# Gate and up matmuls over both parts of x, with other reads and weight loads, in a two-block transformer kernel

## The reference, cut to what matters

```python
def swiglu(x, w_gate, w_up, w_down):
    return (jax.nn.silu(x @ w_gate) * (x @ w_up)) @ w_down
...
    for l in range(DEPTH):
        h = h + 0.5 * swiglu(rmsnorm(h, ffn1_norm[l]), ffn1_w_gate[l], ffn1_w_up[l], ffn1_w_down[l])
        ...
        h = h + 0.5 * swiglu(rmsnorm(h, ffn2_norm[l]), ffn2_w_gate[l], ffn2_w_up[l], ffn2_w_down[l])
```

## Time and profile before

| | us |
|---|---|
| median of 3 runs | 1557.85 |
| lowest, highest | 1557.55, 1558.78 |
| the profiled execution, its own time | 1558.99 |
| span of the profile | 1557.2 |
| TensorE busy | 1538.7 (99%) |
| VectorE busy | 1086.0 (70%) |
| ScalarE busy | 798.4 (51%) |
| mean granted TensorE clock | 0.998 |
| read from HBM | 257.83 MB, 166 GB/s |

### The profile page before, as it was taken

How to read it: one execution, slowest core, us unless ns; L and a number is a source line. 1 busy time by engine, 2 the same in 40 slices (tenths; PEclk the granted TensorE clock), 3 DMA queues, 4 the chain that set the end, 5 groups by cost and what they waited for, 6 DMA issues and landing times.

```text
span 1557.2 us, 29379 instructions
## 1 busy us (share of the span) xinstructions
PE 1538.7 (99%) x12818; PEld 1506.6 (97%) x12818; DVE 1086.0 (70%) x1490; ACT 798.4 (51%) x1029; POOL 44.5 (3%) x43
## 2 busy tenths in 40 slices
PE   7999999999999999999999999999999999999998
PEld 6999999999999999999999999999999999999988
DVE  6665588787875555755568778876688698666844
ACT  5344355565454334533355556444555645775653
POOL 0000001210000000000001010000000000000000
PEclk9999999999999999999999999999999999999999
DMA  7555545434455554555544443446555453325531
GB/s 279 190 185 189 169 153 171 140 132 147 171 198 184 177 183 169 208 180 177 186 153 156 176 136 136 154 171 247 189 182 172 163 190 113 132 82 192 181 129 55
DMA packets 38559, 260.76 MB, mean 167 GB/s; under 512 B 4640, under 2 KB 5024, under 8 KB 8864
## 3 DMA queue, kind: packets, MB, share of 16 engines
q1 hardware_dynamic: 37712, 257.84, 48.0%
q10 hardware_dynamic: 720, 1.05, 0.2%
HBM read 257.83 MB, written 1.05 MB: 166 GB/s over the span
## 4 chain that ended last, share of the span: by engine, by line
PE 92%; DVE 4%; ACT 2%; DMA 1%; issue 0%; ACTq 0%; DVEq 0%
PE ps L203 28%; PE ps L205 28%; PE ps L204 28%; DVE w_low L193 2%; ACT w_high L186 1%; PE ps L1210 1%; DMA w_raw<-in_weights 1%; PE ps L1222 1%; PE ps L1999 0%; PE ps L1982 0%; PE ps L1195 0%; PE ps L1202 0%; PE ps L1194 0%; PE ps L2424 0%; PE ps L1293 0%
## 5 line engine op out<-in xcount | busy, mean ns | idle before, releaser
L193 DVE TENSOR_TENSOR w_low<-w_raw,w_high 128x2048 fp32r<-128x2048 f32 (+2 forms) x245 | 554.6, 2265 | 203.4 <-ACT w_high L186 203.1
L186 ACT ACTIVATE w_high<-w_raw 128x2048 fp32r<-128x2048 f32 (+2 forms) x245 | 460.3, 1880 | 431.9 <-PE ps L205 425.6
L203 PE MATMUL ps<-x_high,w_high 128*128 128x256 f32 x2312 | 662.0, 286 | 11.5 <-DVE w_low L658 9.9
L204 PE MATMUL ps<-x_low,w_high 128*128 128x256 f32 x2312 | 654.7, 283 | 0.0
L205 PE MATMUL ps<-x_high,w_low 128*128 128x256 f32 x2312 | 654.7, 283 | 0.0
L203 PEld LDWEIGHTS ps<-x_high,w_high 128*128 128x128 f32 x2312 | 443.4, 192 | 17.3 <-issue 13.4
L204 PEld LDWEIGHTS ps<-x_low,w_high 128*128 128x128 f32 x2312 | 443.7, 192 | 0.9 <-issue 0.5
L205 PEld LDWEIGHTS ps<-x_high,w_low 128*128 128x128 f32 x2312 | 443.6, 192 | 0.0
L205 PE MATMUL ps<-ffn_hid_high,w_low 128*128 128x256 f32 x704 | 197.9, 281 | 0.0
L203 PE MATMUL ps<-ffn_hid_high,w_high 128*128 128x256 f32 x704 | 197.3, 280 | 0.0
L204 PE MATMUL ps<-ffn_hid_low,w_high 128*128 128x256 f32 x704 | 195.8, 278 | 0.0
(11 more groups left out here) (431 smaller groups left out, 1971.1 us busy)
## 6 DMA issues: line engine op xcount, KB each, us to landing
w_raw<-in_weights SPq DMA_DIRECT2D x230, 1024.0 KB, 4.9
w_raw<-in_weights SPq DMA_DIRECT2D x10, 768.0 KB, 4.2
even_second_vectors<-in_second SPq DMA_DIRECT2D x1, 1836.0 KB, 9.3
w_raw<-in_weights SPq DMA_DIRECT2D x3, 512.0 KB, 3.7
w_raw<-in_weights SPq DMA_DIRECT2D x2, 640.0 KB, 3.9
resid<-in_x SPq DMA_DIRECT2D x4, 256.0 KB, 5.5
w_raw<-in_weights ACTq DMA_DIRECT2D x4, 256.0 KB, 7.2
out<-resid SPq DMA_DIRECT2D x3, 256.0 KB, 2.4
```

What stands on the lines that cost most here:

```text
L186: act.activation(self.wh[:, j, 0:SIZES[n]], self.raw[:, j, 0:SIZES[n]], ACT.Copy).then_inc(self.hi_made, 1)
L193: dve.tensor_tensor(self.wl[:, j, 0:SIZES[n]], self.raw[:, j, 0:SIZES[n]], self.wh[:, j, 0:SIZES[n]].bitcast(F32), ALU.subtract).then_inc( ...
L203: pe.matmul(out, ah, bh, start=start, stop=False, skip_group_check=True)
L204: pe.matmul(out, ah, bl, start=False, stop=False, skip_group_check=True)
```

## The change

Five things are done.

- `x_high` and `x_low` become two halves of one tensor `x`, and gate and up slots use a new `wide`: the high weights move both halves, 512 columns, into a whole bank, and the low weights move `x_high`, 256 columns, into its first half. The two feature halves of a slot take a bank each: gate banks 0 and 1, up banks 2 and 3. The reader (`take_wide`) adds a bank's two halves with a reduce over pairs; the multiply by the scale is an operation of its own behind it, and at step 0 the reciprocal stands between them. The mean of a feed-forward's norm goes to bank 7. The side products of `Tables` wait until up's banks have been read, and their own readers are waited for before the next up (`taken`).
- SyncE issues slot 1 in two halves once the first two pieces of x and slot 0 have landed, and slot 2 once all four have; slot 1 is split in halves.
- In the even layer, at slot 8, `scan` stands ahead of the split.
- The first two output slots of the odd layer run heads 0 to 2 of both, and then head 3 of both.
- A feed-forward's first matmul waits for three residual adds of the unit before, not two.

```diff
-        self.xh = sb("x_high", [P, DT, SEQ], F32R)
-        self.xl = sb("x_low", [P, DT, SEQ], F32R)
+        self.x = sb("x", [P, 2, DT, SEQ], F32R)
+        self.xh, self.xl = self.x[:, 0], self.x[:, 1]
...
-        return n + PIECES
+        return n + PIECES + (n > 0)
...
+def take_wide(c, dve, out, bank):
+    return dve.tensor_reduce(out, c.ps[:, bank:bank + 2, :].rearrange("p f (a t) -> p f t a", a=2), AX.X, ALU.add)
+def wide(c, pe, bank, n, norm=None, midway=None):
+    wh, wl = c.weights_at(n, DT, FC)
+    if n > 1:
+        pe.wait_ge(c.lo_made, c.made(n))
+    for k in range(DT):
+        if midway and k == DT // 2:
+            midway()
+        if norm and k % 2 == 0:
+            pe.wait_ge(*norm.x_low(k // 2 + 1))
+        if n == 0 and k % 2 == 0:
+            pe.wait_ge(c.lo_made, k // 2 + 1)
+        if n == 1 and k % 4 == 0:
+            pe.wait_ge(c.lo_made, PIECES + 1 + k // 4)
+        for i in range(2):
+            f = slice(i * P, (i + 1) * P)
+            pe.matmul(c.bank(bank + i).rearrange("p (a t) -> p a t", a=2), wh[:, k, f], c.x[:, :, k, :], start=(k == 0),
+                      stop=False, skip_group_check=True)
+            mm = pe.matmul(c.bank(bank + i, SEQ), wl[:, k, f], c.xh[:, k, :], start=False, stop=(k == DT - 1),
+                           skip_group_check=True)
+    return mm
...
-B_GATE, B_UP, B_DOWN = (0, 2), 1, 4
+B_GATE, B_UP, B_DOWN, B_FFN_SUM = 0, 2, 4, 7
...
             dve.wait_ge(*self.filled(gate_at(s) + 1))
-            dve.tensor_tensor(b.gate[:, :, :], c.halves(B_GATE[s % 2]), scale, ALU.mult).then_inc(b.gate_read, 1)
+            take_wide(c, dve, b.gate[:, :, :], B_GATE).then_inc(b.gate_read, 1)
+            if s == 0:
+                self.norm.reciprocal(dve)
+            dve.wait_ge(*self.gate_read(s + 1))
+            dve.tensor_tensor(b.gate[:, :, :], b.gate[:, :, :], scale, ALU.mult).then_inc(b.gate_scaled, 1)
         def up(s):
             dve.wait_ge(*self.filled(up_at(s) + 1))
             if s:
                 dve.wait_ge(*self.hid_low(s))
-            dve.tensor_tensor(b.up[:, :, :], c.halves(B_UP), scale, ALU.mult).then_inc(b.up_read, 1)
+            take_wide(c, dve, b.up[:, :, :], B_UP).then_inc(b.up_read, 1)
+            dve.wait_ge(*self.up_read(s + 1))
+            dve.tensor_tensor(b.up[:, :, :], b.up[:, :, :], scale, ALU.mult).then_inc(b.up_scaled, 1)
...
-            if s >= 2:
-                pe.wait_ge(*self.gate_read(s - 1))
-            project(c, pe, B_GATE[s % 2], base + gate_at(s), DT,
-                    norm=None if s else self.norm).then_inc(c.done, 1)
+            if s:
+                pe.wait_ge(*self.gate_read(s))
+            wide(c, pe, B_GATE, base + gate_at(s), norm=None if s else self.norm).then_inc(c.done, 1)
         def up(s):
             if s:
                 pe.wait_ge(*self.up_read(s))
-            project(c, pe, B_UP, base + up_at(s), DT,
-                    midway=None if s else lambda: self.norm.mean(pe)).then_inc(c.done, 1)
+            self.aside.taken(pe, s)
+            wide(c, pe, B_UP, base + up_at(s), midway=None if s else lambda: self.norm.mean(pe)).then_inc(c.done, 1)
...
-            pe.wait_ge(*self.before(2))
+            pe.wait_ge(*self.before(3))
...
-            self.aside.tensor(pe, s)
+            self.aside.tensor(pe, s, self.up_read(s + 1))
...
-        c.load(sp, 1)
+        sp.wait_ge(*self.arrived(1))
+        for b, s in enumerate((self.half_in, c.landed[1])):
+            sp.dma_start(self.half(c.raw, b), c.weights[1][:, b * SLOT // 2:(b + 1) * SLOT // 2]).then_inc(s, 16)
+        sp.wait_ge(*self.arrived(PIECES - 1))
         c.load(sp, 2)
...
-        c.split_high(act, 1)
+        for b, s in enumerate((self.half_in, c.landed[1])):
+            act.wait_ge(s, 16)
+            act.activation(self.half(c.wh, b), self.half(c.raw, b), ACT.Copy).then_inc(c.hi_made, 1)
...
-    def tensor(self, pe, s):
+    def taken(self, pe, s):
+        e = self.e
+        if s == 8:
+            pe.wait_ge(e.skip_made, 4)
+        if s in (9, 10):
+            pe.wait_ge(e.b_copied, s - 8)
+    def tensor(self, pe, s, up_read):
         c, e = self.c, self.e
+        if s in (7, 8, 9):
+            pe.wait_ge(*up_read)
...
-            pe.wait_ge(*((e.b_copied, 1) if part else (e.skip_made, 4)))
...
+            if n == A_Q:
+                scan(A_S5.index(n))
             if n:
                 after(n)
-            if n in A_S5:
+            if n in A_S5 and n != A_Q:
...
+        def heads(n, which):
+            b = odd_bank(n) if which[0] else bank_free(n)
+            wh, wl = c.weights_at(base + n, DT, FC)
+            pe.wait_ge(c.lo_made, c.made(base + n))
+            for h in which:
+                pe.wait_ge(self.o_low, h + 1)
+                for kk in (2 * h, 2 * h + 1):
+                    for i in range(2):
+                        f = slice(i * P, (i + 1) * P)
+                        mm = exact3(pe, c.halves(b)[:, i, :], wh[:, kk, f], wl[:, kk, f], o.oh[:, kk, :], o.ol[:, kk, :],
+                                    kk == 0 and i == 0, kk == DT - 1)
+            return mm
...
+            if n == G_OUT:
+                heads(n, range(3))
+                heads(n + 1, range(3))
+                heads(n, (3,)).then_inc(c.done, 1)
+                heads(n + 1, (3,)).then_inc(c.done, 1)
+                continue
+            heads(n, range(GLA_HEADS)).then_inc(c.done, 1)
```

65 lines of the change are left out of this document (33 added, 32 removed).

## The result

The changed kernel takes **1565.8 us** (median of 5 runs, 1564.1 to 1567.78), the kernel before, beside it, 1557.71. The ratio is 1.0052, with a 95% interval from 1.0037 to 1.0067: slower by 8.1 us, where 5.5 us less were forecast and the range ended at 1561.

A forecast was written before the change was run, and what follows sets the result against it. PE's stream was taken to bound the kernel. Terms: -12.0 - 2.6 - 1.4 + 7.2 + 1.6 + 1.7 + 0 = -5.5 us, giving 1553.5 profiled and 1552.4 for the median; range 1543.5 to 1561.

The forecast's parts named there:

- pairs: Gate and up slots: two 256-column matmuls become one of 512, 1408 times, each saving 8.5 ns; 12.0 us saved.
- even, S5 before the split: Even mixer's slot 8: rotation ahead of the split removes PE's 1.2 us stand and likely 1.6 of slow matmuls; 2.6 us saved.
- odd head: Odd layer: PE's 1.3 us stand for `odd_o_low` goes, hidden behind 36 products of the next slot; 1.4 us saved.
- fourth: the stands: Fourth feed-forward: VectorE falls behind, so PE stands 5.8 us before the S5 products, plus smaller waits; 7.2 us lost.
- fourth: the clock: Fourth feed-forward: after the 6 us stand PE's clock drops and 17 matmuls run slowly; 1.6 us lost.
- third's gate 1: Where one feed-forward follows another: gate 1 now waits for gate 0's read behind two splits; 1.7 us lost, once.
- start: Kernel start: gate 1 begins at 24.8 to 27.6 against 25.49, between 0.7 won and 2.1 lost; taken as 0.
- The price of a read: VectorE: each of 88 bank reads costs 1.22 us more for its reduce, 2.5 us a step; hidden in plain steps.
- D: Rival, chance 0.15: slower because the reduce is dear; at 2.3 us a read the kernel takes 1563.
- B: Rival, chance 0.20: VectorE holds PE nowhere for long, so 12.5 to 14.5 us are won; about 1544.
- C: Rival, chance 0.14: merging two matmuls saves only 2.5 to 5 ns each; sum -0.5 to +3.0, about 1559.
- E: Rival, chance 0.03: 512-column matmuls over two distant pieces start 0.24 us apart, saving nothing; +6.5, 1564.

The follow-up runs named there:

- r4: The kernel before with only the two small parts added: S5 inputs ahead of the even layer's split, last odd head last; 1554.99 us against 1557.74.
- r7: The changed kernel with gate and up of steps 4 to 10 of the fourth feed-forward, and the side products' waits, as before; 1557.28 us.
- r10: The changed kernel with unpaced loads, position and table loads behind slot 4's, and step 0's gate and up reduces ahead of slot 3's split; 1557.33 us.
- r6: The changed kernel with gate and up of the last step of each feed-forward as before, in 256-column matmuls and one multiply as read; 1559.64 us.
- r2: The changed kernel without SyncE's two waits at the start, so slots 1 and 2 are issued at once; 1562.93 us.
- r1: The changed kernel with the reduce of gate 0 ahead of the split of slot 3, in all four feed-forwards; 1560.93 us.
- r9: The changed kernel itself, unaltered, profiled a second time; 1565.86 us (two runs).
- r5: The changed kernel with x_high and x_low of one k-tile side by side, so a 512-column matmul moves one unbroken row; 1567.45 us.
- r3: The changed kernel with the first residual add ahead of VectorE's last split in each feed-forward; 1561.62 us.

## Why the prediction was wrong

The forecast was -5.5 us, the measurement +8.1, outside the range. Each term stands against the traces of the two kernels:

| term | forecast | traces | runs |
|---|---|---|---|
| pairs | -12.0 | -14.7 | |
| even, S5 before the split | -2.6 | -2.3 | r4: -2.75 |
| odd head | -1.4 | -1.8 | (both) |
| fourth: the stands | +7.2 | +6.1 | r7: -8.5 |
| fourth: the clock | +1.6 | +2.6, in part hidden | (with its end) |
| third's gate 1 | +1.7 | +2.2 | r10: -8.5 |
| start | 0 | +6.8 | (both) |
| the feed-forwards' ends | not named | +6.3 | r6: -6.2 |

The traces' terms sum to +5.2; the spans differ by 5.1. The fourth feed-forward's two terms are PE's account of it; since VectorE sets its time behind the stand, they can't be told apart beyond their sum.

**Right.** The price of a read, 1.22 us and 2.5 a step, taken from a reduce of another shape; no row reduced pairs or read its input from PSUM, so that it held is partly luck. What it does in the fourth feed-forward up to the stand: one stand of 5.6 against 5.8, before the S5 products, on up 7's read; the wait in `taken`, 0.8, did not come, while those ahead of gate 7 and up 7, forecast at 0.2 and 0.4, were 0.2 and 0.3. The wait at the third feed-forward's gate 1, 1.8 against 1.7. The two small parts. VectorE hidden in plain steps: the double slots of the first three feed-forwards show no wait for it in between.

**Wrong, first: the start** ("Gate 1 starts at 24.8 to 27.6 against 25.49 ... I take 0"). Gate 1 started at 29.55, 4.1 us later. Two steps failed. Slot 3's split was put between 23.6 and 26.4 because its load was issued earlier; it ended at 28.36, since an earlier place in a busy queue is not an earlier landing, and what had been held back to let the first pieces through was now ahead of it. And the sentence that PE waits elsewhere for the same thing compared the start of gate 1 with before, without asking what a stand of 6 us does to the clock: 2.7 us more, by the same reading of the clock that the prediction made for the fourth feed-forward. r2 puts 2.9 us down to the pacing, r1 shows that the order of VectorE's work is the other part, and r10, with both mended and the tables moved, leaves nothing of it; what the tables' place is worth alone was not run.

**Wrong, second: the ends of the feed-forwards.** The prediction asked of each place whether VectorE's work fits into a step, and wrote of the adds that they cost nothing "as long as VectorE adds in time". It did not follow the chain of the last step, which has no step behind it to catch up in. Its slack was in the trace: `x_low` at 201.94, PE at 202.88. Two reads at 1.26 against 0.94 gives 1.6 by that reading, and 1.6 from start to start was measured, four times. This term alone takes the forecast from -5.5 to +0.8.

**Wrong, but small: two sentences.** "By step 8 VectorE has used the stand to catch up": it had not, as the two profiles of the change show. And the whole difference was "applied to the median": the 1.6 us of slow matmuls in the even layer stand in the profiled execution and in about a quarter of the others, so against the median that term was nearer 1.2 than 2.6. r4 measured 2.75 for it and the odd head's 1.8 together, which leaves about 1.0.

**Mis-sized: the pair.** 8.5 ns, from six matmuls of 512 in a row, against 13 and 7 measured. No row of before showed that there are two paces, and a figure from six starts of 0.01 us could not have told them apart. The upper bound of 17.6 us covers it in total. The estimate of 3.5 us that the prediction made from the Trainium skill (TensorE: Matmul & The Clock Gate, section Back-to-back issue gap) is too small here: two gate and up slots lost 0.41 or 0.22 us where 32 pairs at 2.5 ns are 0.08. The section gives that formula for a matmul by itself and not for a stream, so it was the wrong one to take.

**The rivals.** D (slower, 1563, through a dear reduce) had the right sign and nearly the time by luck, with the wrong cause: the reduce was as priced, and other places had less slack than counted. B, C and E fall. What was missing is a rival for slower in which VectorE's price is as forecast and the places are more: every place where a read became part of a chain.

What stays open is why a feed-forward runs at 11.10 or at 11.29, and what made the 1.7 us by which the first profile of the change stands below its median; r9's, with nine double slots more at the slow pace, stands 0.2 below. The layout of x is excluded (r5), and the granted clock was 1.00 in both.

## What to carry to other kernels

When an operation on a busy but not limiting engine gets longer, don't only ask whether its work fits into a period: at every place where the loop ends or begins, lay out the chain from its result to the next thing the limiting engine asks for, and read the slack there, which here was 0.9 us against 2.5 added. Fewer buffers (gate's two banks in turn became one pair) make the read of a buffer urgent, so move reads ahead of all that waits for a load. And a load that is issued earlier behind held-back traffic can land later: hold back what is needed last (the tables), not what is needed next.

## What was not expected of the hardware

- PE runs one and the same stream of 512- and 256-column matmuls at one of two paces, 0.347 or 0.353 us a pair, at a granted clock of 1.00; it keeps one for most of a feed-forward, and the same kernel took the second feed-forward at either (11.11 and 11.30 us for two slots). The stream before, all of 256 columns, showed one pace only, 11.51 to 11.52, outside the fourth feed-forward's last three steps. In every profile of the wide kernels the fourth feed-forward was at the slow one before its S5 products.
- A reduce over pairs from PSUM, 1024 elements to 512, takes what one of 1024 elements from SBUF to 16 takes: 1.223 and 1.219 us. What the two have in common is the number of elements read.
- A stand of PE of 1.4 to 1.5 us at the feed-forwards' ends left the granted clock at 1.00, while one of 1.2 in the even layer of the kernel before was followed by 0.61; a stand of 3.9 in r1 was followed by 0.70 to 0.73, those of 5.6 and 5.9 by 0.50 for 6 us. The length of the stand alone does not say it, nor does its place: the stand of 1.7 to 1.8 at the third feed-forward's gate 1 left the clock at 1.00 in both profiles of the change, and in r3, the same there, it was followed by 0.67 and 0.76, which cost 1.3 us.

```profile
639.00:642.00 3.00, 2.65 (x15) 2.33 (x16) 2.97 (x4) 0.84 (x2) 0.00 (x0) 1.00 0.99 399
...
639.00:642.00 3.00, 2.25 (x7) 1.93 (x8) 2.97 (x4) 0.96 (x1) 0.00 (x0) 0.67 1.00 412
```

The first row is the changed kernel's, the second r3's.
